# Two stages of an fp32 layer pair move to three rounded products, and the rows of a third product move to ScalarE and GpSimd

## Chip, core and metric

One core of one Trainium2 chip. The metric is the device time of one execution of the kernel in microseconds (us), median of several runs; lower is better. The kernel before took 2692.47 us (2692.26 to 2692.58 in 3 runs).

## The reference, cut to what matters

The kernel computes three stacked layers in fp32 for 256 tokens of width 2048. Only the first layer is touched:

```
mod = silu(c) @ w_ada + b_ada                      # 1 x 6144
shift, scale, gate = split(mod, 3)
h = rms_norm(x) * (1 + scale) + shift              # 256 x 2048
xr, gr, qc, kvc, kr, ga = split(h @ w_in)          # xr, gr, ga: 1024 wide each
y_rnn = rg_lru_branch(xr, ...) * silu(gr)
y_att = mla_branch(qc, kvc, kr, ...) * silu(ga)    # 8 heads
x = x + gate * (concat(y_rnn, y_att) @ w_out)
```

Two later layers (a differential attention and a stick-breaking attention, each with a convolutional feed-forward) follow and are the same in both kernels. They take the stretch from about 455 us to the end.

## The kernel before, in words

Everything lies transposed: features on the 128 partitions, 256 tokens along the row. `xm` is h in the reference's sense (16 tiles of 128 features x 256 tokens, fp32), `h` is the residual stream x, of the same size.

**Units.** Weights arrive in units of 4 x 128 rows by 256 columns (512 KB, 128 partitions x 1024 numbers). In the first layer each unit lies in a ring of 8 places `w1`; TensorE multiplies it as plain fp32 (helper `two_tiles`, L838 to L846, and the loop at L1032 to L1042): 8 matmuls of 128x128 weights by 128x256 activations. The profile shows an fp32 matmul as two records. The units run in this order, counted by the semaphore `w1_used`: up to unit 39 the modulated latent products and three quarters of the recurrent products; units 40 to 43 the last quarter of xr (L995 to L998); units 44 to 57 the fourteen pairs of heads of the latent attention, `U_PAIRS` (nope, rope, knope, v; L1002 to L1011); units 58 to 61 the last quarter of gr; units 62 to 77 the attention gate ga, four groups of four units. From unit 58 on, after each unit comes `attention(slot)` (L1014), which puts in a head's scores, turns and outputs, and in slots 3 and 19 `gate_sums` (L982).

In all later products a unit is split instead: ScalarE copies it rounded (`hi`, L1367), VectorE subtracts the copy from it (L1841), and TensorE takes high times high, high times low and low times high, in type float32r. The first split units are those of `w_out` (`residual_product`, L1115 and L1173), right behind unit 77. Their wide form lets one matmul of 512 columns carry two of the three products.

**Gate rows.** The gate third of `mod` isn't needed before `w_out`'s results are added up. It is made on VectorE in 32 rows (`gate_row`, L2131): one row is 128 of the 2048 rows of w_ada by 1024 columns, loaded by SyncE's queue into one of the four places of `raw` (`gate_load`, L542; it waits until the row 4 before has been used), and VectorE multiplies it by silu(c) of its partition and adds it to `gate_sum` in one instruction (L2144, L2141 for the first of each half). After 16 rows `gate_sums` adds up over the partitions on TensorE with 8 matmuls (L989), then `gate_sum` is used again for the other half.

**Queues.** Each engine runs its instructions in the order written. ScalarE (L1455 to L1581) takes in the pairs: the logarithm and exponential of the roots of the pair before (L1416, L1418), the squares of this pair (L1496), for v a copy (L1498) and the sigmoids of the recurrent gates (L1483). VectorE (L2148 to L2279) has the latent outputs, four convolutions (`conv`, L2109), `rnn_in` (L2097), heads (L2121), gate rows between them; then per head the maxima, a step of the recurrence, the weights of the head, two gate rows. GpSimd does nothing after two kinds of memsets at the start (L666, L668). SyncE's queue issues all loads in the order of use.

The lines that set the path of the pairs are these three waits of TensorE:

```
two_tiles(halves(take(U_BANK[n], read=(F.heads_out.sem, 2 + n) ...)), ...)   # a bank is free again
head_sums(n - 1)                                                             # waits for ScalarE's squares of pair n-1
recurrent_gates(g)                                                           # waits for ScalarE to have read scores and turned
```

Of the kernel before, what the change touches and what calls it, by code (L numbers as in the profile page):

```python
# [16 lines left out]
F32 = mybir.dt.float32  # L17
# [64 lines left out]
for _n in range(ONE_UNITS):  # L82
    _lora = _n < XR_AT and not any(q <= _n < q + 8 for q in QUARTER_AT)
    _size = LORA_COLS if _lora else UK * 256
    if _n == ONE_UNITS - 8:
        _at = ONE_SPACE // 2
    if _at + _size > ONE_SPACE:
        _at = 0
    ONE_SPAN.append((_at, _at + _size))
    _at += _size  # L90

ONE_FREE = [max([m + 1 for m in range(n) if ONE_SPAN[m][0] < ONE_SPAN[n][1] and ONE_SPAN[n][0] < ONE_SPAN[m][1]]
                + [n - ONE_RING + 1, 0]) for n in range(ONE_UNITS)]
# [136 lines left out]
def splits(units):  # L230
# [8 lines left out]
     "ada_product"]  # L239
# [4 lines left out]
class FirstBlock:  # L244


    def __init__(self, sems):
# [3 lines left out]
         self.pack_in, self.ada_product, *slots) = [Tally(s) for s in sems]  # L251
# [20 lines left out]
FIRST_SLOT = 2  # L272
# [34 lines left out]
def program(nc, t, out, consts):  # L307

    ctx = ExitStack()
    with ctx:  # L310
# [17 lines left out]
        h = sb("h", [KT, TOK])  # L328
        begin_at("weights_gap", WEIGHTS_STEP)
        wr_at = nc.sbuf_base  # L330
        wr = sb("wr", [2, SLOT_PAIR], F32R)
        w1 = nc.alloc_sbuf_tensor_at("w1", [P, ONE_SPACE], F32, offset=-(-wr_at // 32) * 32)
# [36 lines left out]
        xm = nc.alloc_sbuf_tensor_at("xm", [P, KT, TOK], F32, offset=xs_at)  # L369
        half = nc.alloc_sbuf_tensor_at("half", [P, KT, TOK], F32, offset=xs_at + KT * TOK * 4)  # L370
        gate_sum = nc.alloc_sbuf_tensor_at("gate_sum", [P, GATE_COLS], F32, offset=xs_at + KT * TOK * 4)
# [23 lines left out]
        rgw = o("rgw", [2, 8, P])  # L395
        p1 = [o(f"p{e}", [3 * P]) for e in range(2)]
# [55 lines left out]

        def lora_rows(n):

            return w1[:, ONE_SPAN[n][0]:ONE_SPAN[n][0] + LORA_COLS]
# [17 lines left out]
        def _(sp):  # L473
# [33 lines left out]
            ada_loads, one_units, gate_loads = [0], [0], [0]  # L507
# [34 lines left out]
            def gate_load():  # L542

                n = gate_loads[0]
                gate_loads[0] += 1
                if n >= RING:
                    sp.wait_ge(T.gate_used.sem, n - RING + 1)
                r, c = n % KT, 2 * D + (n // KT) * GATE_COLS
                sp.dma_start(raw[:, n % RING, :], w_ada[r * P:(r + 1) * P, c:c + GATE_COLS])\
                  .then_inc(F.gate_in[n % RING].sem, 16)  # L550

# [34 lines left out]
            sp.wait_ge(F.rgw_zeroed.sem, 1)  # L586
            for m, name in enumerate(("w_rg_a", "w_rg_x")):
                for b in range(2):
                    r = slice(64 * b, 64 * b + 64)
                    sp.dma_start(rgw[r, m, :, r], t[name][0].rearrange("(t b) i j -> b i t j", b=2)[b])\  # L590
                      .then_inc(T.rgw_in.sem, 16)
            for i in range(4):
                quarter_load(i, 3)
            for what, g in U_PAIRS:
# [8 lines left out]
                gate_load()  # L603
            for i in range(4):
                quarter_load(4 + i, 3)
                gate_load()
            for n in range(N_GA):
                pair_load(GA + 256 * (n // 4), n % 4)
                if n < GATE_LOADS - N_U - 4:
                    gate_load()  # L610
# [19 lines left out]
            for n in range(8):  # L630
                cols = slice(n * 256, (n + 1) * 256)
                pair(w_out, cols)

# [29 lines left out]
        def _(pool):  # L663
            F = FirstBlock(first_sems)
# [3 lines left out]
            pool.memset(rgw[:, :, :, :], 0.0).then_inc(F.rgw_zeroed.sem, 1)  # L668


        @block.tensor
        def _(pe):
# [174 lines left out]

            def halves(b):
# [133 lines left out]
            def gate_sums(step):  # L982
# [5 lines left out]
                for m in range(n):  # L988
                    mm = pe.matmul(sums[:, step * n + m:step * n + m + 1], gate_sum[:, m * P:(m + 1) * P], ones[:, 0:1],  # L989
# [10 lines left out]
            pe.wait_ge(T.rgw_in.sem, 64)  # L1000

            for n, (what, g) in enumerate(U_PAIRS):  # L1002
                if g == 0:
# [10 lines left out]
            def attention(slot):  # L1014
# [8 lines left out]
                if slot == 3:  # L1023
                    gate_sums(0)
                if slot == 19:
# [3 lines left out]
            for i in range(4):  # L1029
                two_tiles(halves(take(GR_BANK[i])), xm, 3 * UK)  # L1030
# [1591 lines left out]
```

## Time and profile before

| | before |
|---|---|
| median of 3 runs | 2692.47 us |
| the profiled execution, its own time | 2691.99 us |
| its span, first to last instruction | 2689.8 us |
| busy: PE / DVE / ACT / POOL | 2679.5 / 1977.5 / 1197.8 / 5.7 us |
| DMA, mean share of 16 engines | 64% of the span, 528 MB |

PE is TensorE, DVE VectorE, ACT ScalarE, POOL GpSimd, SP SyncE; a name with q behind it is the engine's queue of DMA issues. L12 is line 12 of the kernel before. The profiled execution's time holds 2.2 us around the span. Durations of matmuls overlap in the rows, since they are pipelined: what one costs is read from start to start.

### The profile page before, as it was taken

The page shows a single profiled execution, that of the slowest core. Times are in us where ns is not written, and L with a number is a line of the kernel's source. Part 1 is how long each engine was busy: PE and PEld are TensorE (multiplying, and loading weights), DVE is VectorE, ACT ScalarE, POOL GpSimd, SP SyncE. Part 2 cuts the span into 40 slices and gives each one's busy share as a digit, 9 for nine tenths or more (in the row PEclk, how much of TensorE's full clock was granted, in tenths as well). Part 3 has the DMA queues.
Part 4 walks back from the last instruction along what each step waited for, and adds up shares of the span by engine and source line. Part 5 has one row for each costly group of instructions (what it writes and reads, how often), then busy time and mean ns, then how long its engine had stood idle before and what let it go on. Part 6 is the DMA issues. An engine that isn't in the chain of part 4 may idle for free.

```text
span 2689.8 us, 44167 instructions
## 1 busy us (share of the span) xinstructions
PE 2679.5 (100%) x15336; PEld 2348.9 (87%) x15336; DVE 1977.5 (74%) x2594; ACT 1197.8 (45%) x1533; POOL 5.7 (0%) x12
## 2 busy tenths in 40 slices
PE   9999999999999999999999999999999999999999
PEld 7888888888888888888888888888888888888888
DVE  6747577777777788667787776699878876688865
ACT  2004354555555444444444443366544444444443
POOL 0000000000000000000000000000000000000000
PEclk9999999999999999999999999999999999999999
DMA  9986665555556666666666666644566666666664
GB/s 342 366 278 191 205 192 191 165 174 163 160 164 196 188 195 190 198 190 195 189 194 188 196 200 190 188 157 140 181 188 195 196 191 192 192 190 195 196 202 155
DMA packets 705780, 528.18 MB, mean 196 GB/s; under 512 B 32221, under 2 KB 694559, under 8 KB 705439
## 3 DMA queue, kind: packets, MB, share of 16 engines
q1 hardware_dynamic: 701872, 523.73, 63.9%
q10 hardware_dynamic: 3823, 3.31, 0.4%
q8 instruction: 54, 0.88, 0.1%
q14 instruction: 31, 0.25, 0.0%
HBM read 523.80 MB, written 2.10 MB: 196 GB/s over the span
## 4 chain that ended last, share of the span: by engine, by line
PE 97%; DVE 2%; ACT 1%; issue 0%; DMA 0%; DVEq 0%; SPq 0%; ACTq 0%
PE acc L707 80%; PE acc L845 3%; PE acc L1039 2%; PE acc L833 2%; PE turned L845 2%; PE sums L845 2%; PE mixed L960 1%; PE sums L1191 1%; DVE pro_ada L1915 0%; DVE wr L1841 0%; PE scores L1184 0%; PE sums L745 0%; PE mixed L961 0%; PE sums L916 0%; PE scores L946 0%
## 5 line engine op out<-in xcount | busy, mean ns | idle before, releaser
L707 PE MATMUL acc<-stream,wr 128*128 128x512 f32 (+1 forms) x7680 | 1328.4, 333 | 0.3 <-DVE wr L1841 0.3
L707 PEld LDWEIGHTS acc<-stream,wr 128*128 128x128 f32 x7680 | 1159.1, 188 | 156.0 <-issue 3.8
L1841 DVE TENSOR_TENSOR wr<-raw,wr 128x1024 fp32r<-128x1024 f32 x832 | 998.5, 1222 | 318.2 <-ACT wr L1367 308.6
L1367 ACT ACTIVATE wr<-raw 128x1024 fp32r<-128x1024 f32 x832 | 871.1, 1058 | 693.8 <-PE acc L707 678.1
L707 PE MATMUL acc<-ys,wr 128*128 128x512 f32 (+1 forms) x4264 | 732.4, 332 | 1.0 <-DVE wr L1841 0.9
L707 PEld LDWEIGHTS acc<-ys,wr 128*128 128x128 f32 x4264 | 642.7, 188 | 85.3 <-DVE wr L1841 1.5
L707 PE MATMUL acc<-wr,stream 128*128 128x512 f32 (+1 forms) x1024 | 182.7, 338 | 0.0
L707 PEld LDWEIGHTS acc<-wr,stream 128*128 128x128 f32 x1024 | 157.0, 188 | 22.5 <-issue 0.5
L1725 ACT ACTIVATE ffn_cv<-ffn_cv 128x256 f32<-128x256 f32 x88 | 36.9, 419 | 245.4 <-DVE ffn_cv L2459 245.4
L1851 DVE TENSOR_REDUCE ffn_ug<-acc 128x512 f32<-128x1024 f32 x88 | 107.8, 1225 | 35.3 <-PE acc L707 35.3
L1874 DVE TENSOR_TENSOR ys<-tmp,ys 128x256 f32 (+3 forms) x108 | 51.2, 474 | 76.0 <-ACT ys L1373 73.4
L1915 DVE SCALAR_TENSOR_TENSOR pro_ada<-aring,small,pro_ada 128x512 f32<-128x512 f32 (+1 forms) x103 | 85.7, 832 | 24.3 <-DMA aring<-in_w_ada 18.3
L1851 DVE TENSOR_REDUCE S<-acc 128x512 f32<-128x1024 f32 x71 | 86.6, 1220 | 12.1 <-PE acc L707 12.1
L1373 ACT ACTIVATE ys<-tmp 128x256 f32 (+3 forms) x104 | 46.8, 450 | 106.3 <-DVE tmp L2463 102.0
L1855 DVE TENSOR_TENSOR ffn_ug<-ffn_ug,rx 128x512 f32<-128x512 f32 x88 | 60.9, 692 | 3.0
L833 PE MATMUL acc<-xm,w 128*128 128x256 f32 x256 | 58.2, 381 | 0.4 <-DVE xm L1935 0.4
L1039 PE MATMUL acc<-xm,w 128*128 128x256 f32 x256 | 57.3, 379 | 0.0
L833 PEld LDWEIGHTS acc<-xm,w 128*128 128x128 f32 x256 | 48.2, 190 | 8.3 <-issue 1.9
L1039 PEld LDWEIGHTS acc<-xm,w 128*128 128x128 f32 x256 | 47.7, 190 | 6.0
L2457 DVE SCALAR_TENSOR_TENSOR ffn_cv<-ffn_ug,vcol,ffn_cv 128x256 f32<-128x256 f32 x88 | 42.7, 485 | 13.2 <-DVE ffn_cv L2454 13.0
L2459 DVE SCALAR_TENSOR_TENSOR ffn_cv<-ffn_ug,vcol,ffn_cv 128x256 f32<-128x256 f32 x88 | 42.7, 485 | 13.0 <-DVE ffn_cv L2457 12.8
L2454 DVE TENSOR_SCALAR ffn_cv<-ffn_ug,vcol 128x256 f32<-128x256 f32 x88 | 36.3, 413 | 16.6 <-DVE ffn_ug L1855 16.4
(334 smaller groups left out, 1546.1 us busy)
## 6 DMA issues: line engine op xcount, KB each, us to landing
raw<-in_ffn_w_up SPq DMA_DIRECT2D x704, 256.0 KB
raw<-in_ffn_w_down SPq DMA_DIRECT2D x160, 512.0 KB
raw<-in_a_w_qkv SPq DMA_DIRECT2D x96, 512.0 KB
raw<-in_b_w_kv SPq DMA_DIRECT2D x64, 512.0 KB
aring<-in_w_ada SPq DMA_DIRECT2D x96, 256.0 KB, 6.6
w<-in_w_in SPq DMA_DIRECT2D x48, 512.0 KB
raw<-in_w_ada SPq DMA_DIRECT2D x32, 512.0 KB, 5.1
raw<-in_w_out SPq DMA_DIRECT2D x32, 512.0 KB
```

The lines of the kernel that those rows point to most:

```text
L707: mm = pe.matmul(*ops, start=first and ops is wide, stop=last and ops is wide)
L833: pe.matmul(bank(c // 2)[:, (c % 2) * TOK:(c % 2 + 1) * TOK], w[:, c * P:(c + 1) * P], xm[:, k, :], start=False, stop=k == KT - 1 and c % ...
L845: mm = pe.matmul(out(j), *here, start=k == 0, stop=k == UK - 1)
L1039: mm = pe.matmul(bank(b + j)[:, 0:TOK], w[:, k, j * P:(j + 1) * P], xm[:, u * UK + k, :], start=u == 0 and k == 0, stop=u == 3 and k == UK ...
L1367: f(half_of(0, s), raw[:, s, :], ACT.Copy)\
L1373: f(to[0], to[1], ACT.Copy).then_inc(T.hi_out.sem, 1)
L1841: tt(half_of(1, s), raw[:, s, :], half_of(0, s), ALU.subtract).then_inc(T.unit_split[s].sem, 1)
L1851: dve.tensor_reduce(out_tiles, a[:, 0:tiles, :].rearrange("p t (b c) -> p t c b", b=2), axis=AX_X, op=ALU.add)\
L1855: tt(out_tiles, out_tiles, both(rx), ALU.mult).then_inc(*T.acc_read.one())
L1874: tt(to[:, :, TOK:2 * TOK], src, to[:, :, 0:TOK], ALU.subtract).then_inc(*T.lo_out.one())
L1915: stt(here, aring[:, n % ADA_RING, 0:2 * kn * P], small[:, 8 + r:9 + r], here, ALU.mult, ALU.add)\
L2457: step(stt(cv[e][:, :], UG[e][:, 1, 1:1 + TOK], taps[1], cv[e][:, :], ALU.mult, ALU.add))
```

## The change

1. The products of units 58 to 77 (last quarter of gr, whole ga) are made from three rounded products of 128x256 each, 24 float32r matmuls a unit instead of 8 fp32 ones. ScalarE makes the rounded copy of each unit (`high`), VectorE the rest (`low`, written over the unit itself). The activations are split too: `xm_high` (4 instructions of ScalarE) and `xm_low` (4 of VectorE, written over `xm`).
2. `xm_high` takes the place of `h`. So `h` is stored to memory (2 MB, on ScalarE's queue, which waits for the landing) and fetched back by SyncE's queue in four pieces, behind units 74 to 77.
3. The gate rows leave VectorE. GpSimd issues their loads (from unit 32 on), ScalarE scales each row in place (7 ahead of the latent squares, then 2 with each pair, 1 less at the end), GpSimd adds it to one of two `gate_sum` tiles, waits for its own addition, and issues the load of the row 4 further on. `gate_sums` move to slots 0 and 10.
4. The recurrent weights are loaded behind unit 50 rather than before unit 40; VectorE's first convolution moves up; the first split slot of `w_out` is 0 rather than 2.

The places of `w1` from unit 58 on are five for units and three for the rounded copies. The core of the diff:

```diff
-for _n in range(ONE_UNITS):
+for _n in range(GR_AT):
...
+LOW_PLACES, HIGH_PLACES = [5, 6, 0, 1, 2], [7, 4, 3]
+ONE_FREE = [max(users_of(ONE_SPAN[n], n) + [n - ONE_RING + 1, 0]) for n in range(ONE_UNITS)]
+HIGH_FREE = [max(users_of(HIGH_SPAN[n], n)) if n >= GR_AT else 0 for n in range(ONE_UNITS)]
...
-FIRST_SLOT = 2
+FIRST_SLOT = 0
...
         @block.gpsimd
+            pool.wait_ge(F.w1_used.sem, XR_AT - 7)
+            def gate_load(n):
+                r, c = n % KT, 2 * D + (n // KT) * GATE_COLS
+                pool.dma_start(raw[:, n % RING, :], t["w_ada"][0][r * P:(r + 1) * P, c:c + GATE_COLS])\
+                    .then_inc(F.gate_in[n % RING].sem, 16)
+            for n in range(RING):
+                gate_load(n)
+            for n in range(GATE_LOADS):
+                r = n % KT
+                here = gate_sum[n // KT][:, :]
+                pool.wait_ge(F.gate_scaled.sem, n + 1)
+                if r:
+                    w = pool.tensor_tensor(here, here, raw[:, n % RING, :], ALU.add)
+                else:
+                    w = pool.tensor_copy(here, raw[:, n % RING, :])
+                w.then_inc(T.gate_used.sem, 1)
+                pool.wait_ge(T.gate_used.sem, n + 1)
+                if n + RING < GATE_LOADS:
+                    gate_load(n + RING)
...
         @block.tensor
+            def three_products(out, high, low, j, k, k0, first, last):
+                cols = slice(j * P, (j + 1) * P)
+                x_high, x_low = xm_high[:, k0 + k, :], xm_low[:, k0 + k, :]
+                pe.matmul(out, high[:, k, cols], x_high, start=first, stop=False)
+                pe.matmul(out, high[:, k, cols], x_low, start=False, stop=False)
+                return pe.matmul(out, low[:, k, cols], x_high, start=False, stop=last)
...
-                if slot == 3:
+                if slot == 0:
                     gate_sums(0)
-                if slot == 19:
+                if slot == 10:
                     gate_sums(1)
...
         @block.scalar
-                        act.wait_ge(F.w1_used.sem, ONE_UNITS if s < FIRST_SLOT else ONE_UNITS - 4)
+                        act.wait_ge(F.w1_used.sem, ONE_UNITS - 2 if s < RING // 2 else ONE_UNITS)
...
+            act.wait_ge(F.w1_used.sem, QUARTER_AT[2])
+            act.dma_start(h_kept, h[:, :, :]).then_inc(F.h_kept.sem, 16)
+            act.wait_ge(F.h_kept.sem, 16)
+            act.wait_ge(F.xm_ready.sem, KT)
+            for u in range(4):
+                f(xm_high[:, u * UK:(u + 1) * UK, :], xm[:, u * UK:(u + 1) * UK, :], ACT.Copy).then_inc(F.high_ready.sem, 1)
+            def gate_scale(count):
+                for _ in range(count):
+                    n = gate_rows[0]
+                    gate_rows[0] += 1
+                    act.wait_ge(F.gate_in[n % RING].sem, 16 * (n // RING + 1))
+                    f(raw[:, n % RING, :], raw[:, n % RING, :], ACT.Copy, scale=small[:, 8 + n % KT:9 + n % KT])\
+                        .then_inc(F.gate_scaled.sem, 1)
+            gate_scale(7)
+            def high(count=1):
+                for _ in range(count):
+                    n = high_units[0]
+                    high_units[0] += 1
+                    act.wait_ge(F.w1_in[n % ONE_RING].sem, UNIT * (n // ONE_RING + 1))
+                    act.wait_ge(F.w1_used.sem, HIGH_FREE[n])
+                    f(high_tiles(n), unit_tiles(n), ACT.Copy).then_inc(F.high_out.sem, 1)
...
                 if what != "v":
                     f(flat(sq[n % 2][:, :, :]), bank(U_BANK[n]), ACT.Square).then_inc(F.sq_ready.sem, 1)
+                    gate_scale(2)
...
+                    if n < N_U - 1:
+                        gate_scale(2 if g < 2 else 1)
             gates(3)
+            high()
...
         @block.vector
-                elif n:
-                    gate_row()
-                if n >= N_U:
-                    gate_row()
+                    tt(low_tiles(n), unit_tiles(n), high_tiles(n), ALU.subtract).then_inc(F.low_out.sem, 1)
...
-                gate_row()
-                gate_row()
+                low(2 if hd < 7 else 1)
...
+            dve.wait_ge(F.h_back.sem, 4 * 16)
             residual_product(gated=True, gain=VEC["attn_norm_g_2"])
```

## Rows read from the trace of the kernel before

**Rows 1.** Busy us by stretch: PE, PEld, DVE, ACT, POOL, clock, DMA share, GB/s.

```profile
207.00:270.00 63.00, 63.00 (x270) 50.95 (x269) 45.15 (x64) 26.04 (x46) 0.00 (x0) 1.00 0.69 210
288.00:367.00 79.00, 79.00 (x397) 65.62 (x396) 55.52 (x103) 32.08 (x69) 0.00 (x0) 1.00 0.59 188
```

**Rows 2.** PE in order of time, attention gate: one unit is 16 records.

```profile
304.90 3.62 PE L1039 MATMUL acc<-xm,w 128*128 128x256 f32 x16
308.35 0.59 PE L960 MATMUL mixed<-one_pT,one_v 128*128 128x256 f32 x2
```

**Rows 3.** PE in order of time at the kernel's end: float32r matmuls of 256 columns.

```profile
2671.20 0.28 PE L733 MATMUL acc<-wr,ys 128*128 128x256 f32 x1
...
2672.14 0.28 PE L735 MATMUL acc<-wr,ys 128*128 128x256 f32 x1
```

**Rows 4.** Groups by line, whole kernel: the splitting of a unit on DVE and ACT.

```profile
L1841 DVE TENSOR_TENSOR wr<-raw,wr 128x1024 fp32r<-128x1024 f32 x832 | 998.5, 1222 | 318.2 <-ACT wr L1367 308.6
L1367 ACT ACTIVATE wr<-raw 128x1024 fp32r<-128x1024 f32 x832 | 871.1, 1058 | 693.8 <-PE acc L707 678.1
```

**Rows 5.** Groups by line on POOL, shapes kept apart; and DVE's gate rows.

```profile
L668 POOL MEMSET one_rgw<- 128x2048 f32 x1 | 1.8, 1810 | 17.9 <-PE turned L778 17.9
L666 POOL MEMSET pro_ada<- 128x1024 f32 x1 | 1.0, 958 | 0.0
...
L2144 DVE SCALAR_TENSOR_TENSOR gate_sum<-raw,small,gate_sum 128x1024 f32<-128x1024 f32 x30 | 38.5, 1282 | 4.0 <-DMA raw<-in_w_ada 2.5
```

**Rows 6.** DMA issues by line (KB each, us to landing), and two issues on SP's queue.

```profile
raw<-in_w_ada SPq DMA_DIRECT2D x32, 512.0 KB, 5.1
...
230.82 0.34 SPq L549 DMA_DIRECT2D raw<-in_w_ada  x1
...
269.06 0.94 SPq L549 DMA_DIRECT2D raw<-in_w_ada  x1
```

**Rows 7.** ACT, DVE and PE in order of time where the latent squares are made.

```profile
173.26 0.73 DVE L1935 TENSOR_SCALAR xm<-xm,mod 128x256 f32<-128x256 f32 x2
...
188.50 1.08 ACT L1457 ACTIVATE sq<-acc 128x512 f32<-128x512 f32 x2 [104.30 <-PE scores L835]
...
191.76 1.89 PE L906 MATMUL mixed<-sq,ones 128*128 128x256 f32 x8
```

**Rows 8.** ACT and PE in order of time in the pairs of heads.

```profile
210.09 0.60 ACT L1496 ACTIVATE sq<-acc 128x512 f32<-128x512 f32 x1 [6.42 <-PE acc L845]
...
223.02 0.69 ACT L1416 ACTIVATE rs<-sums,epsc 128x512 f32<-128x512 f32 x1 [1.37 <-PE sums L916]
223.74 0.63 ACT L1418 ACTIVATE rs<-rs 128x512 f32<-128x512 f32 x1
224.28 0.58 ACT L1496 ACTIVATE sq<-acc 128x512 f32<-128x512 f32 x1
...
266.15 0.84 ACT L1483 ACTIVATE ri<-scores,vcol 128x256 f32<-128x256 f32 x2 [0.27 <-PE scores L978]
...
222.82 3.62 PE L845 MATMUL acc<-qx,w 128*128 128x256 f32 x16
...
227.13 3.62 PE L845 MATMUL acc<-qx,w 128*128 128x256 f32 x16
...
270.26 1.03 PE L978 MATMUL scores<-xc,one_rgw 128*128 128x256 f32 x4
```

**Rows 9.** DVE and PE in order of time at the fourth pair's bank.

```profile
217.58 0.69 DVE L2097 TENSOR_TENSOR xrp<-acc,half 128x512 f32<-128x512 f32 x1
...
218.51 3.62 PE L845 MATMUL acc<-qx,w 128*128 128x256 f32 x16
```

**Rows 10.** PE in order of time behind the attention gate, and one more stretch of busy time.

```profile
367.41 1.84 PE L989 MATMUL sums<-ones,gate_sum 128*128 128x1 f32 x16
369.12 26.14 PE L707 MATMUL acc<-ys,wr 128*128 128x512 f32 x152
...
145.00:188.00 43.00, 43.00 (x209) 38.07 (x208) 20.54 (x34) 0.00 (x0) 0.00 (x0) 1.00 0.87 270
```

More of the change, by code:

```diff
@@ L90, with users_of @@
     _at += _size
-ONE_FREE = [max([m + 1 for m in range(n) if ONE_SPAN[m][0] < ONE_SPAN[n][1] and ONE_SPAN[n][0] < ONE_SPAN[m][1]]
-                + [n - ONE_RING + 1, 0]) for n in range(ONE_UNITS)]
+LOW_PLACES, HIGH_PLACES = [5, 6, 0, 1, 2], [7, 4, 3]
+HIGH_SPAN = [None] * GR_AT
+for _n in range(ONE_UNITS - GR_AT):
+    for _spans, _place in ((ONE_SPAN, LOW_PLACES[(_n + 2) % 5]), (HIGH_SPAN, HIGH_PLACES[_n % 3])):
+        _spans.append((_place * UK * 256, (_place + 1) * UK * 256))
+def users_of(span, n):
+    return [m + 1 for m in range(n) for used in (ONE_SPAN[m], HIGH_SPAN[m])
+            if used and used[0] < span[1] and span[0] < used[1]]
+ONE_FREE = [max(users_of(ONE_SPAN[n], n) + [n - ONE_RING + 1, 0]) for n in range(ONE_UNITS)]
+HIGH_FREE = [max(users_of(HIGH_SPAN[n], n)) if n >= GR_AT else 0 for n in range(ONE_UNITS)]
 XR_BANK, U_BANK, GR_BANK = [None, None, 0, 1], [(n + 2) % 4 for n in range(N_U)], [0, 1, 2, 3]
@@ L585, in _ @@
                 lora_load(k)
[L586 to L591, printed above, removed]
             for i in range(4):
                 quarter_load(i, 3)
-            for what, g in U_PAIRS:
+            for n, (what, g) in enumerate(U_PAIRS):
                 if what in ("nope", "rope"):
@@ L999, in _ @@
             rope_turn(kpe[:, :], 1, 0)
-            pe.wait_ge(T.rgw_in.sem, 64)
             for n, (what, g) in enumerate(U_PAIRS):
+                if what == "v" and g == 0:
+                    pe.wait_ge(T.rgw_in.sem, 64)
                 if g == 0:
@@ L1029, in _ @@
             for i in range(4):
-                two_tiles(halves(take(GR_BANK[i])), xm, 3 * UK)
+                out = halves(take(GR_BANK[i]))
+                high, low = split_unit()
+                for j in range(2):
+                    for k in range(UK):
+                        mm = three_products(out(j), high, low, j, k, 3 * UK, k == 0, k == UK - 1)
+                mm.then_inc(F.w1_used.sem, 1)
                 attention(i)
@@ L1491, in _ @@
                     act.preload_act_table(ACT.Sigmoid)
+                if n == N_U - 1:
+                    high(2)
                 if what == "v" and g:
@@ L2127, in rope_out, with xm_lows, low @@
                             F.mixed_ready, F.mixed_read))
-            gate_rows = [0]
-            def gate_row():
-                n = gate_rows[0]
-                gate_rows[0] += 1
-                r = n % KT
-                if n == KT:
-                    dve.wait_ge(T.gate_summed.sem, 1)
-                dve.wait_ge(F.gate_in[n % RING].sem, 16 * (n // RING + 1))
-                c = small[:, 8 + r:9 + r]
-                if r == 0:
-                    w = ts(gate_sum[:, :], raw[:, n % RING, :], c, None, ALU.mult)
-                else:
-                    own(T.gate_used)
-                    w = stt(gate_sum[:, :], raw[:, n % RING, :], c, gate_sum[:, :], ALU.mult, ALU.add)
-                w.then_inc(*T.gate_used.one())
+            def xm_lows(u):
+                tiles = slice(u * UK, (u + 1) * UK)
+                dve.wait_ge(F.high_ready.sem, u + 1)
+                tt(xm_low[:, tiles, :], xm[:, tiles, :], xm_high[:, tiles, :], ALU.subtract)
+            low_units = [GR_AT]
+            def low(count=1):
+                for _ in range(count):
+                    n = low_units[0]
+                    low_units[0] += 1
+                    dve.wait_ge(*F.high_out.next())
+                    tt(low_tiles(n), unit_tiles(n), high_tiles(n), ALU.subtract).then_inc(F.low_out.sem, 1)
+            for u in range(3):
+                xm_lows(u)
             lora_out("q")
             rnn_in(0)
+            conv(0)
             lora_out("kv")
+            rnn_in(1)
             rope_key()
-            conv(0)
-            rnn_in(1)
             dve.wait_ge(T.table_ready.sem, 4)
@@ L2246, in _ @@
             F.scores_ready.n, F.scores_read.n = 8, 8
-            for i in range(4):
+            for i in range(3):
+                low()
                 rnn_gate(i)
```

73 lines of the change are left out of this document (50 added, 23 removed).

## The prediction

> **What bounds the kernel now.** I read the busy time by stretch first [rows 1]: TensorE is busy in every microsecond of the two stretches the change touches (63.00 of 63 us in the pairs of heads, 79.00 of 79 in the attention gate, clock 1.00), while VectorE has 45.15 and 55.52, ScalarE 26.04 and 32.08 and GpSimd nothing. So TensorE's own work is the path, and the others matter where they make it wait. Then the order of time on TensorE [rows 2, 3] for the price of a product, the groups by line [rows 4, 5] and the DMA issues [rows 6] for the price of what is added, and the order of time on ScalarE beside TensorE [rows 7, 8] for how late ScalarE may be before TensorE waits.
>
> **The product.** A plain unit runs from 304.90 to the next operation's start at 308.35: 3.45 us for 8 fp32 matmuls, 0.43 each [rows 2]. Float32r matmuls of 256 columns with new weights each stand at the end of the kernel: 8 steps from 2671.20 to 2672.14, 0.118 us each [rows 3]. Three products are 24 of them a unit: 2.83 us. Twenty units (58 to 77) give 20 x 0.62 = **-12.5 us**, all on the path, since TensorE has no idle time there. The ends: 0.118 is of the same shape and type, so no better; if the new places in the memory read more slowly, at worst the whole gain is gone (0).
>
> **What carries the splits.** ScalarE's rounded copy takes 1.06 us, VectorE's subtraction 1.22 [rows 4]. In the attention gate (15 of the 20 units' splits fall there, the others earlier) ScalarE gets 32.1 + 15 x 1.06 = 48 us, VectorE 55.5 - 15 gate rows x 1.28 [rows 5] + 15 x 1.22 = 54.6 us, both in a stretch that shrinks to some 69. Both fit. TensorE has two units of lead on the splits, so a wait comes from order only: I take +1. The sums of the gate's second half (1.7 us from 367.41 to 369.12 [rows 10]) move to slot 10 and cost the same there, but no longer cover the first splits of the output product: +1. Together **+2** (0 to 4).
>
> **The gate rows** are the doubtful part. Their 32 instructions leave VectorE, which was not the bound: worth nothing by itself. In their place each row passes ScalarE (1.06 us in the queue that makes the squares TensorE waits for), then GpSimd's addition, then GpSimd's issue of the load four rows on, then 5.1 us to landing [rows 6]. The ring has four places, and ScalarE's `gate_scale` waits for the landing with squares, roots and sigmoids queued behind it. So the number that decides is c, GpSimd's time per row, addition plus issue. No row shows either. The nearest: GpSimd writes 1024 numbers per partition in 0.958 us (2048 in 1.81) [rows 5]. An addition reads two streams and writes one: 0.96 if all overlap, 2.87 if they come one behind the other. The issue: SyncE's queue takes 0.34 us for the same transfer free of pressure and 0.94 with it [rows 6]. c lies between 1.3 and 3.8. I take three streams in a row and the free issue, 2.87 + 0.34 = **3.2**: the same instruction on VectorE, the faster engine for it in these rows, already takes 1.28 with two inputs, so full overlap on GpSimd is unlikely.
>
> *First wait.* `xm` is complete at 173.26 + 0.73 = 174.0 [rows 7]; four copies of xm take ScalarE to 178.2, row 0 is scaled by 179.3. GpSimd issues rows 4, 5, 6 at 3.2 us each (row 0 is a copy, one stream or 0.96 less): row 6 at 187.9, landed 193.0, scaled 194.1. The latent squares started at 188.50, so they are 5.6 late. They took 1.08, and TensorE asked at 191.76 [rows 7]: 2.2 of cover. Price **+3.4**.
>
> *The pairs.* One pair lasts 4.31 us on TensorE (222.82 to 227.13) [rows 8]. ScalarE's own part is 0.72 + 0.63 + 0.58 us (starts 223.02, 223.74, 224.28) and now two scalings, 2.12: 4.05 of 4.31, so ScalarE alone still keeps up. GpSimd needs 6.4 us for the two rows, and it stood still before, because row 7 is only scaled behind the squares of pair 0: those ended at 210.7 [rows 8], with the shift 214.1, row 7 scaled at 215.2. Row 31's load is issued after 21 additions (rows 7 to 27): 215.2 + 21 x 3.2 = 282.4, less 0.96 for row 16, a copy: 281.4. Landed 286.5, scaled 287.6, and behind it the first sigmoid of the recurrent gates (0.84 us; it began at 266.15) ends at 288.4. TensorE's next gates stood at 270.26 [rows 8], with the shift 273.7. Price **+15**, seen as waits of some 2 us in nearly each pair. It is late at squares first, then at sigmoids.
>
> **Shared port.** GpSimd's additions now run beside VectorE's convolutions. VectorE's `rnn_in` for the bank of the fourth pair ended at 218.27, TensorE took the bank at 218.51 [rows 9]: 0.24 us of cover, some 2 more from the convolution moved up. If VectorE must let additions pass there (at most two, 2 x 2.87), it costs 0 to 6; no gain, since nothing here frees VectorE before that point. I take **+3**, the middle. The Trainium skill, page SBUF — State Buffer, section "Who interferes with whom", says that a VectorE instruction with two SBUF inputs and a GpSimd instruction that reads SBUF block each other for the whole instruction, whoever comes second; by it the top end counts, without it 0. No row here has both engines at it.
>
> **At nothing.** The store of `h` (2 MB) and four early row loads fall between 143 and 172 us, where DMA is at 0.87 and 270 GB/s [rows 10]: 4 MB are some 13 us of transfers against 43 x 0.13 = 5.6 us free, but the loads there run two to five units ahead of TensorE, which hides them (0 to +3 if not). ScalarE waits for the store's landing, but was idle for 104.30 us before 188.50 [rows 7]. `xm_high` and `xm_low` (4 x 1.06, 3 x 1.22) fall into the same idle time. The four issues that fetch `h` stand on SyncE's queue ahead of the loads of `w_out`'s second columns; these are needed four units, 11 us, later, and 2 MB take about 7. The recurrent weights' four issues move behind unit 50, over 20 us ahead of their use. If that cover is gone it is 1 to 2 us once.
>
> **Sum.** -12.5 + 2 + 3.4 + 15 + 3 = +10.9. Against the profiled execution (2691.99, of which 2689.8 are span) that is 2702.9; the median is 0.5 above that execution: 2703.
>
> **Rivals.** A measurement of this kernel tells some 0.2% (5.4 us) from no change.
>
> *A, faster: the ring keeps up.* Each 0.1 us of c weighs 24 x 0.1 = 2.4 us, and the sum is zero at c = 3.2 - 10.9 / 24 = 2.75; below 2.5 it is faster by over 0.2%. With c = 1.3 row 6 is scaled within the 2.2 us of cover and nothing waits: -12.5 + 2 = -10.5, or 2682. For it: GpSimd's writing is as quick as ScalarE's copy. Against: two inputs. With VectorE undisturbed and c about 1.9, 2683. Chance 0.24.
>
> *B, no change.* GpSimd's addition takes twice VectorE's 1.22 [rows 4], the issue 0.34: c = 2.8, -9.6 on the forecast, 2693. Chance 0.15. The page GPSIMD Engine Reference, section 3.1, gives 4497 ns for such an addition of 2048 numbers, an estimate of 2.25 us for 1024; with the issue as above, c would be 2.6 and the time 2689. The same skill's page DMA: Bandwidth & Descriptors, section "Latency and other measured facts", gives about 1 us until the first byte of a transfer issued by GpSimd, which would bring c back to 3.3. No row here shows either.
>
> *C, slower still.* The issue costs as much as SyncE's under pressure, c = 3.8: +1.8 at the first wait, +12.6 in the pairs, and the port's top end, +3: 2720. Half-way lies the case that the three products don't bring what they say, for the places of `xm_high` and the copies read more slowly: at worst +12.5, 2715. Chance 0.19.
>
> Forecast (c from 2.9 to 3.6, 2698 to 2713): 0.42.
>
> **How the numbers follow.** Faster is A, 0.24; same is B, 0.15; slower is the forecast and C, 0.61. The range goes from A's likely end, 2683, to just above C's, 2722; about a tenth is left on each side. The forecast's own range is 2698 to 2713.
>
> **What would show it.** On TensorE, units 58 to 77 start 2.83 us apart where no attention lies between. GpSimd's start-to-start time from one addition to the next between 215 and 280 us is c. ScalarE's scalings show idle time ended by the rows' DMA; TensorE waits for ScalarE at L916 in most pairs, and at L978. VectorE's convolutions show whether they wait beside GpSimd. I am wrong if c is under 2.7, if ScalarE's waits stay inside TensorE's cover, or if units 58 to 77 take over 3 us.

## The result, and the profile after

| | before | after |
|---|---|---|
| median | 2692.51 us (4 runs) | 2707.95 us (2707.05 to 2710.44, 4 runs) |
| ratio to before | | 1.0058, interval 1.0046 to 1.0071 |
| the profiled execution, and its span | 2691.99, 2689.8 us | 2708.8, 2707.0 us |
| busy PE / DVE / ACT / POOL | 2679.5 / 1977.5 / 1197.8 / 5.7 us | 2676.6 / 1990.9 / 1255.3 / 97.8 us |

The change makes the kernel 15.4 us slower; 2703 was forecast, with 2683 to 2722 as the range. In the experiments below one execution of e3 (7382.36 us) and one of e10 (3339.08 us) were slow; the medians given for these two include it and would otherwise be 2686.86 and 2697.69 us.

Busy time by stretch in the kernel after (columns as in [rows 1]):

```profile
207.00:270.00 63.00, 52.22 (x207) 40.35 (x205) 45.29 (x45) 35.49 (x46) 45.10 (x32) 0.95 0.78 228
220.00:226.00 6.00, 0.87 (x3) 0.04 (x1) 5.93 (x4) 0.51 (x1) 5.66 (x4) 0.99 0.83 269
226.00:232.00 6.00, 4.35 (x10) 3.50 (x11) 4.28 (x7) 2.36 (x4) 0.68 (x2) 0.50 0.38 121
276.00:282.00 6.00, 0.53 (x3) 0.13 (x1) 0.75 (x1) 4.79 (x7) 5.36 (x5) 0.87 0.51 150
282.00:286.00 4.00, 3.71 (x9) 3.02 (x10) 0.00 (x0) 2.52 (x5) 3.58 (x3) 0.50 0.65 198
290.00:370.00 80.00, 79.41 (x571) 71.51 (x570) 52.65 (x89) 52.58 (x98) 7.18 (x3) 0.98 0.46 134
```

In the pairs of heads TensorE, busy without a gap before [rows 1], now lacks 10.8 of 63 us. Two holes stand out, 220 to 226 and 276 to 282, and behind each the granted clock is 0.50, the 1.2 GHz level. From 290 us on, where the three products run, hardly anything is lost: the clock of 0.98 there is a fall to 0.66 between 346 and 350 us, and the version without rows (e4 below) has the same fall at 322 to 326 us. So the loss lies in the pairs, as forecast. The list of waits between 150 and 400 us (us in total, times, longest) names what TensorE waited for:

```profile
PE acc L892 <- DVE xrp L2203: 6.8, 1, 6.8
PE scores L1040 <- ACT ri L1580: 5.8, 1, 5.8
PE sums L978 <- ACT sq L1595: 4.2, 2, 2.3
PE mixed L968 <- ACT sq L1554: 1.4, 1, 1.4
PE acc L906 <- DVE w_split L2250: 1.0, 2, 0.5
PE acc L754 <- DVE wr L1947: 0.6, 2, 0.3
ACT raw L1537 <- DMA raw<-in_w_ada: 18.2, 13, 2.6
```

The last row is the ring of four rows: ScalarE's scaling stood 13 times for a transfer, 18.2 us in all. What sets the pace of the ring is GpSimd's order of time in the pairs (start, us, operation):

```profile
238.48 0.57 POOL L699 DMA_DIRECT2D raw<-in_w_ada  x1 [0.30 <-POOL gate_sum L709]
239.08 2.37 POOL L709 TENSOR_TENSOR gate_sum<-gate_sum,raw 128x1024 f32<-128x1024 f32 x1
241.74 0.57 POOL L699 DMA_DIRECT2D raw<-in_w_ada  x1 [0.30 <-POOL gate_sum L709]
242.34 2.36 POOL L709 TENSOR_TENSOR gate_sum<-gate_sum,raw 128x1024 f32<-128x1024 f32 x1
```

One row costs 2.37 for the addition, 0.30 in which GpSimd stands before it issues the next load, and 0.57 for the issue: c = 3.26 us from start to start, where 3.2 was taken. The first entry of the waits, though, is VectorE's. This is the convolution ahead of it, beside TensorE, in order of time:

```profile
210.83 2.71 DVE L2215 SCALAR_TENSOR_TENSOR xc<-xrp,vcol,xc 128x256 f32<-128x256 f32 x6
213.65 0.69 DVE L2203 TENSOR_TENSOR xrp<-acc,half 128x512 f32<-128x512 f32 x1
214.38 2.46 DVE L2213 TENSOR_SCALAR xc<-xrp,vcol 128x256 f32<-128x256 f32 x2
216.88 9.93 DVE L2215 SCALAR_TENSOR_TENSOR xc<-xrp,vcol,xc 128x256 f32<-128x256 f32 x6
226.90 0.69 DVE L2203 TENSOR_TENSOR xrp<-acc,half 128x512 f32<-128x512 f32 x1
...
227.65 6.19 PE L892 MATMUL acc<-qx,w 128*128 128x256 f32 x16 [6.78 <-DVE xrp L2203]
233.68 1.02 PE L978 MATMUL sums<-sq,ones 128*128 128x512 f32 x2
```

The same six instructions take 2.71 us at 210.83, while GpSimd waits for a row, and 9.93 at 216.88, while it adds. `xrp` comes 9.3 us later than in [rows 9], TensorE stands 6.78 us, and its next unit lasts 6.03 us from start to start (227.65 to 233.68) in place of 3.45: 2.58 more for the clock. The second hole costs 5.76 and then 2.54 (7.72 from 282.29 to 290.01 for what takes 5.18 from there to 295.19). With the other waits that is 19.8 of waiting and 5.1 of clock.

VectorE is behind one more of these waits, although the list names ScalarE's squares for it. The convolution after that one, on VectorE, ScalarE and TensorE:

```profile
232.62 9.51 DVE L2215 SCALAR_TENSOR_TENSOR xc<-xrp,vcol,xc 128x256 f32<-128x256 f32 x6
242.06 0.74 DVE L2227 SCALAR_TENSOR_TENSOR one_qn<-acc,vcol,rs 128x512 f32<-128x512 f32 x1
242.89 0.69 ACT L1483 ACTIVATE rs<-sums,epsc 128x512 f32<-128x512 f32 x1 [4.24 <-DVE one_qn L2227]
244.15 0.58 ACT L1595 ACTIVATE sq<-acc 128x512 f32<-128x512 f32 x1
244.78 1.13 PE L978 MATMUL sums<-sq,cst 128*128 128x512 f32 x2 [2.32 <-ACT sq L1595]
```

The head's output `one_qn` stands behind the stretched convolution, ScalarE waits 4.24 us for it before it takes the next root, the squares stand behind that root, and TensorE waits 2.32 us. ScalarE waits for no row's transfer between 191.6 and 252 us. Its waits for transfers come again from 252 us on, ahead of the other wait at the squares (1.90 us at 270.22) and of the 5.76 at the sigmoids.

### The profile page after: what moved, and what is told of

Same layout as the page of the kernel before. It is cut to its first block, busy times and chain, and to the rows that moved or that the text cites. A ratio compares the mean times of both kernels' runs of the same rounds, so it can differ in the third digit from the quotient of the medians.

```text
span 2707.0 us, 44576 instructions
## 1 busy us (share of the span) xinstructions
PE 2676.6 (99%) x15496; PEld 2349.5 (87%) x15496; DVE 1990.9 (74%) x2586; ACT 1255.3 (46%) x1589; POOL 97.8 (4%) x76
## 4 chain that ended last, share of the span: by engine, by line
PE 92%; DVE 4%; ACT 1%; POOL 1%; issue 1%; DMA 1%; DVEq 0%; SPq 0%; ACTq 0%; POOLq 0%
PE acc L754 80%; PE sums L892 2%; PE turned L892 1%; PE acc L880 1%; POOL gate_sum L709 1%; DVE xc L2215 1%; PE mixed L1022 1%; PE sums L1258 1%; PE acc L892 1%; PE acc L906 0%; DVE wr L1947 0%; PE acc L908 0%; PE acc L907 0%; PE scores L1251 0%; PE sums L792 0%
## 5 line engine op out<-in xcount | busy, mean ns | idle before, releaser
L1957 DVE TENSOR_REDUCE S<-acc 128x512 f32<-128x1024 f32 x71 | 86.7, 1221 | 11.7 <-PE acc L754 11.7
L709 POOL TENSOR_TENSOR gate_sum<-gate_sum,raw 128x1024 f32<-128x1024 f32 x30 | 71.8, 2394 | 19.6 <-ACT raw L1537 18.7
L880 PE MATMUL acc<-xm,w 128*128 128x256 f32 x256 | 58.3, 380 | 0.4 <-DVE xm L2041 0.4
L880 PEld LDWEIGHTS acc<-xm,w 128*128 128x128 f32 x256 | 48.2, 190 | 8.3 <-issue 1.9
L2250 DVE TENSOR_TENSOR w_split<-w,w_split 128x1024 fp32r<-128x1024 f32 x20 | 27.0, 1381 | 35.0 <-ACT w_split L1550 35.0
```

The source lines that it names most:

```text
L709: w = pool.tensor_tensor(here, here, raw[:, n % RING, :], ALU.add)
L880: pe.matmul(bank(c // 2)[:, (c % 2) * TOK:(c % 2 + 1) * TOK], w[:, c * P:(c + 1) * P], xm[:, k, :], start=False, stop=k == KT - 1 and c % ...
L1957: dve.tensor_reduce(out_tiles, a[:, 0:tiles, :].rearrange("p t (b c) -> p t c b", b=2), axis=AX_X, op=ALU.add)\
```

## Experiments

They ran in three groups, each beside the kernel before on the same chip (2692.4 to 2692.5). Two theories stood against each other. **Ring:** only the time of a row counts, through the landing of the row four places on. **Port:** GpSimd's addition also holds up VectorE's instructions with two operands from SBUF. Where a version is told as e1, e2 and so on, that is its number below.

**e4: no rows (what the products alone are worth).** 30 of the 32 rows are neither loaded, scaled nor added (the attention's gate is left out of the result).

```diff
-            gate_scale(7)
+            gate_scale(2)
...
-                    gate_scale(2)
-                        gate_scale(2 if g < 2 else 1)
```

> Thirty of the 32 gate rows are left out (their loads, scalings and additions; the two rows left are copied). What stays is the three products, the split of the activations, the store and return of h, the moved loads. All theories on the rows: 2680 to 2684, the products' 12.5 us less some 1 to 3 for order and tail. If 2690 or more, the products or the store of h cost more than I think and the rows' part is smaller.

Measured: 2682.88 us (2682.45 to 2685.5), ratio 0.9965 (0.9953 to 0.9978). TensorE's whole list of waits between 150 and 400 us is:

```profile
PE acc L899 <- DVE w_split L2240: 1.1, 2, 0.6
PE acc L747 <- DVE wr L1937: 0.6, 2, 0.3
```

So the rows and what carries them cost 25.1 us in the changed kernel (2707.95 - 2682.88). In the two profiled executions the difference is 24.1 (2708.8 - 2684.74), and the waits (19.8 - 1.7) with the clock (5.1) give 23.2 of it.

**e8: the kernel before without the rows.** The control for e4: 30 of 32 rows left out of the kernel before, in loads and sums.

```diff
             def gate_row():
                 n = gate_rows[0]
                 gate_rows[0] += 1
+                if n % KT:
+                    return
```

> The kernel before with 30 of its 32 gate rows left out, loads and sums (the gate of attention is left out of the result). If the rows hide completely beside the fp32 products, it takes 2692 us as before, and the 9.5 us between before and the version of the changed kernel without rows are the worth of the products alone. If the rows and their loads cost something there, it is faster by that, up to 2 us, and the products are worth so much less.

Measured: 2692.34 us (2691.93 to 2692.78), ratio 0.9999 (0.9990 to 1.0008). On VectorE, beside fp32 products, the rows were free, and the three products with all that goes with them are worth 9.5 us (2692.4 - 2682.9).

**e1: GpSimd only writes.** The addition becomes memsets of 1024, 1024 and 256 numbers, which read nothing (the gate is left out of the result).

```diff
-                    w = pool.tensor_tensor(here, here, raw[:, n % RING, :], ALU.add)
+                    pool.memset(raw[:, n % RING, :], 0.0)
+                    pool.memset(here, 0.0)
+                    w = pool.memset(scratch[:, :], 0.0)
```

> GpSimd's additions become three memsets of 1024, 1024 and 256 numbers (about 2.2 us by its memset rows, 2.4 for the addition), which write and read nothing; what is left out is the sum itself. GpSimd's time per row stays about 3.1 us, so the ring of rows is as slow as before the edit. Theory ring (ScalarE waits for rows, TensorE for ScalarE, and that is the whole loss): 2703 to 2706, nearly all of the loss stays. Theory port (GpSimd's reading blocks VectorE's convolutions, and that is the loss): VectorE's convolution group L2215 back at 2.7 us from 9.9, TensorE's wait of 6.8 us for xrp gone, 2681 to 2685. Theory both in a row: the 6.8 us and some 2.5 us of slow clock behind it go, the waits at squares and sigmoids grow by part of that, 2695 to 2700.

Measured: 2694.73 us (2693.68 to 2696.94), ratio 1.0010 (1.0000 to 1.0019), at 2.93 us a row: next to the range of "both", far from the other two. Groups by line between 170 and 300 us, VectorE's convolutions:

```profile
L2218 DVE SCALAR_TENSOR_TENSOR xc<-xrp,vcol,xc 128x256 f32<-128x256 f32 x24 | 10.6, 482 | 0.4
L2216 DVE TENSOR_SCALAR xc<-xrp,vcol 128x256 f32<-128x256 f32 x8 | 4.6, 616 | 0.1
```

The 24 instructions take 10.6 us in all, as in the kernel before; no wait for `xrp` is left, and the clock is 1.00 from 207 to 290 us. GpSimd was busy for 62.46 of those 83 us, more than in e2 below (55.67). So it isn't GpSimd's being busy that holds VectorE up. (The second row, 4.6 in place of 2.9 before, shows that one kind is slowed by writes as well: see the last section.)

**e2: ScalarE doesn't scale.** GpSimd waits for the transfer itself, so ScalarE is out of the ring (the scale is left out of the result).

```diff
-                pool.wait_ge(F.gate_scaled.sem, n + 1)
+                pool.wait_ge(F.gate_in[n % RING].sem, 16 * (n // RING + 1))
```

> ScalarE scales no row (left out: the product with silu(c)); GpSimd waits for the landing itself and adds, 3.26 us a row, in one run from about 165 us on. Theory ring: no wait of TensorE at squares or sigmoids is left, 2682 to 2686. Theory port: the additions now run beside all four convolutions from 199 us on, the wait for xrp stays at 6 to 9 us or comes earlier, 2690 to 2695. Both: 2690 to 2695, with all that is left of the loss at waits for VectorE.

Measured: 2720.43 us (2719.44 to 2720.86), ratio 1.0102 (1.0085 to 1.0119). With less work than the changed kernel it is 12.5 us slower. GpSimd and VectorE of this kernel in order of time (starts 3.25 us apart for the additions):

```profile
201.48 2.36 POOL L711 TENSOR_TENSOR gate_sum<-gate_sum,raw 128x1024 f32<-128x1024 f32 x1
204.14 0.57 POOL L699 DMA_DIRECT2D raw<-in_w_ada  x1 [0.30 <-POOL gate_sum L711]
204.72 2.37 POOL L711 TENSOR_TENSOR gate_sum<-gate_sum,raw 128x1024 f32<-128x1024 f32 x1
...
201.11 9.90 DVE L2217 SCALAR_TENSOR_TENSOR xc<-xrp,vcol,xc 128x256 f32<-128x256 f32 x6
210.94 1.65 DVE L2184 SCALAR_TENSOR_TENSOR kvx<-acc,vcol,rs 128x256 f32<-128x256 f32 x4
212.51 0.67 DVE L2205 TENSOR_TENSOR xrp<-sums,half 128x512 f32<-128x512 f32 x1
```

Three additions pass during the six instructions (9.90 = 3 x 3.25, nearly), so two of the six go with each addition. Taken one by one they last 3.02, 0.47, 2.82, 0.47, 2.81 and at most 0.5 us: one passes in the gap of 0.89 us between additions, and the next, which starts before the addition (at 204.56 ahead of 204.72, the first at 201.11 ahead of 201.48), lasts until the addition is over. The additions themselves stay at 2.36 us. The instructions behind them, which take one operand from an accumulator bank, run beside the next addition at their usual 0.41 and 0.67 us. The theory of the ring alone falls here: the ring had lost ScalarE's part and the kernel went up. TensorE's waits were 11.4 us for `xrp`, 8.2 for `sq` and 6.8 for `kpe`; behind that `sq` ScalarE had waited 12.18 us for `one_qn`, after a convolution of 11.99. The forecast of the port had only the time wrong (2690 to 2695).

**e3: a copy in place of the addition.** One operand read in place of two.

```diff
-                if r:
-                    w = pool.tensor_tensor(here, here, raw[:, n % RING, :], ALU.add)
-                else:
-                    w = pool.tensor_copy(here, raw[:, n % RING, :])
+                w = pool.tensor_copy(here, raw[:, n % RING, :])
```

> GpSimd copies each scaled row (one operand read, one written) in place of adding it to the sum (two read, one written): the gate of attention is left out of the result. The changed kernel showed such a copy at 1.05 us against 2.37 us for an addition, so a row should take 1.05 + 0.30 + 0.57 = 1.9 us. Theory ring (only the time of a row counts): the ring keeps up, 2684 to 2687 us. Theory port (GpSimd holds up VectorE's instructions with two operands whenever it reads): the copies still hold VectorE up, but for 1.05 of every 1.9 us and only while rows are in work; six of the convolution's instructions in a row take between 2.7 and 7 us, and the kernel 2685 to 2692 us. If only an instruction of GpSimd with two operands read holds VectorE up, the six take 2.7 us as in the kernel before.

Measured: 2686.88 us, ratio 0.9979 (0.9969 to 0.9989). GpSimd and VectorE in order of time:

```profile
223.27 1.04 POOL L708 COPY gate_sum<-raw 128x1024 f32<-128x1024 f32 x1 [1.96 <-ACT raw L1534]
225.13 1.05 POOL L708 COPY gate_sum<-raw 128x1024 f32<-128x1024 f32 x1
227.07 1.22 POOL L708 COPY gate_sum<-raw 128x1024 f32<-128x1024 f32 x1
...
223.34 5.22 DVE L2212 SCALAR_TENSOR_TENSOR xc<-xrp,vcol,xc 128x256 f32<-128x256 f32 x6
```

A single operand read is enough: the six take 5.22 us, 2.5 more than undisturbed, beside copies that fill 1.05 of every 1.9 us. The stretch falls where "any read" had put it, and "only two operands read" is out. The time doesn't tell the theories apart, since 2686.88 lies in the ranges of both ring and port. In TensorE's waits the port doesn't show directly: 1.3 us at the sigmoids and 0.4 at the squares, and ScalarE had waited 1.11 us for a row's transfer ahead of the latter.

**e7: SyncE issues the loads.** GpSimd's row loses its 0.57 us of issue; all else is as changed.

```diff
-                if n + RING < GATE_LOADS:
-                    gate_load(n + RING)
...
         @block.sync
+                gate_loads_before(n + 1)
```

> The changed kernel, but SyncE issues the loads of the gate rows in place of GpSimd: a row costs GpSimd 2.37 + 0.30 us instead of 3.26 us. Theory ring: at 2.7 us a row the ring nearly keeps pace and ScalarE's rows come in time, 2686 to 2693 us. Theory port: GpSimd now adds for 2.37 of every 2.7 us while rows are in work, VectorE's convolutions take at least as long as in the changed kernel (six in a row 9 us or more), TensorE waits again for xrp or qn, and the kernel takes 2700 to 2712 us.

Measured: 2705.85 us (2702.63 to 2707.11), ratio 1.0045 (1.0030 to 1.0060). The convolution of the third quarter in VectorE's order of time:

```profile
215.08 4.63 DVE L2227 TENSOR_SCALAR xc<-xrp,vcol 128x256 f32<-128x256 f32 x2
219.75 6.76 DVE L2229 SCALAR_TENSOR_TENSOR xc<-xrp,vcol,xc 128x256 f32<-128x256 f32 x6
226.61 0.69 DVE L2217 TENSOR_TENSOR xrp<-acc,half 128x512 f32<-128x512 f32 x1
```

The row got shorter than expected: where GpSimd doesn't wait for a row its additions start 2.43 us apart (180.85, 183.28, 185.71), although it still waits for its own addition, so the 0.30 us belong to the issue behind it. By the forecast's own rate (2.4 us for each 0.1 us of c) 0.83 less should have brought some 20 us; 2.1 came. `xrp` is done at 227.3, 0.3 us earlier than in the changed kernel. With the gap between additions gone, VectorE's place to slip through is gone too: beside additions in a row each of its instructions lasts about one addition (2.19 and 2.52 for the first two here), and the next convolution takes 11.06 us. TensorE waits 5.8 us for `xrp` and 4.4 for squares that stand behind that next convolution. The forecast of the port holds (2700 to 2712), though the six at this place took 6.76, not 9 or more.

**e10: writes only, but longer rows.** e1 with one more wait inside the row.

```diff
-                    pool.memset(raw[:, n % RING, :], 0.0)
+                    pool.memset(raw[:, n % RING, :], 0.0).then_inc(F.pool_step.sem, 1)
+                    pool.wait_ge(F.pool_step.sem, n - n // KT)
```

> As the version in which GpSimd only writes (three memsets for an addition, 2.93 us a row, 2694.7 us), with one more wait inside each row, so that a row takes the 3.25 us of the changed kernel and still reads nothing (the gate of attention is left out). Theory ring alone: the row's time is all that counts, 2704 to 2710 us. Theory both (the ring and the reads): 0.3 us more on some 25 rows is at most 8 us, 2698 to 2703 us, and the rest to 2708 us is what GpSimd's reads do to VectorE, with the slower clock that follows. TensorE's clock stays at full speed and no wait for xrp appears in either version without reads.

Measured: 2697.91 us (2696.33 at the lowest), ratio 1.0020 (1.0010 to 1.0029). My setting missed its mark: a row took 3.05 us (217.90, 220.94, 223.99 in GpSimd's order of time), not 3.25, for a wait on GpSimd's own signal costs about 0.1 us where no issue follows. The rate from e1 to here is 3.2 us for 0.12, or 2.7 for each 0.1, close to the forecast's 2.4. Carried on to 3.26 at 2.4 it gives 2703, which is an extrapolation. One expectation was wrong: the clock did fall here (0.96 from 207 to 290 us), behind waits for `sq` of up to 3.2 us, with no read of GpSimd's anywhere.

**e5, e6, e9: the products kept, the rows back on VectorE.** These compute all that the reference asks. e5 puts VectorE's own row instruction (scaled and added in one, 1.28 us) at two a pair, with SyncE's loads among the units:

```diff
-            gate_scale(7)
...
+                elif n:
+                    gate_row(1 if n < 3 else 2)
```

> Complete kernel: the products as changed, the rows again one fused instruction of VectorE each (1.28 us), but two with each pair from the fifth on, one behind each of the first three lows and heads; loads on SyncE's queue four rows ahead; ScalarE and GpSimd have no part in them. Ring and port theories alike: both causes are gone, 2681 to 2686, faster than both kernels. If VectorE is now too full, it shows as waits of TensorE for low_out or for heads, 2690 to 2700.

Measured: 2690.10 us, ratio 0.9994 (0.9984 to 1.0003): 18 us better than the change, and no better than before. The forecast was missed; TensorE's waits were 3.7 us at the sigmoids and 1.4 for the transfer of `w_uq`. e6 takes six rows ahead of the latent sums and gives five to the heads:

```diff
             for u in range(3):
                 xm_lows(u)
+            gate_row(6)
...
-                    gate_row(1 if n < 3 else 2)
+                    gate_row(2 if 3 < n < 8 else 1)
```

> As the version with the rows back on VectorE (2690.1 us), but with six rows done by VectorE right after the low parts of xm, where it stood idle for 16 us and the DMA engines had nothing to do for 20 us a little later, and fewer rows beside the units of the value heads, where the DMA engines had been busy all the time. If late transfers are the 7 us that separated that version from the one without rows (2682.9 us), it takes 2683 to 2686 us, and TensorE waits neither for w_uq nor for the recurrent gates. If VectorE's own time is the cost, it stays at 2688 to 2691 us.

Measured: 2688.06 us (2686.5 to 2688.89), ratio 0.9983 (0.9974 to 0.9992): half a miss. The wait for the gates was gone, but the one for `w_uq` was not (1.8 us), and the heads had a new one of 1.4. SyncE's order of time showed why: it stood ahead of `w_uq` until VectorE freed a row's place at 219.3 us. e9 issues the rows one unit later there and moves two rows from the heads to the pairs:

```diff
-            rows_by = [6, 7, 8, 8, 10, 12, 14, 16] + [17 + i for i in range(11)] + [27, 28]
+            rows_by = [6, 6, 7, 8, 10, 12, 14, 16, 18, 20] + [21 + i for i in range(8)]
```

> As the last version with the rows on VectorE (2688.1 us), in which TensorE still waited 1.8 us for w_uq, because SyncE stood at the load of a row whose place VectorE freed only at 219.3 us, and 1.4 us for a head's probabilities, where VectorE had five rows among the heads. Here SyncE issues the rows one unit later, and two rows move from the heads to the pairs. If these two waits are the difference, it takes 2684 to 2686 us; if the rows cost something that no wait of TensorE shows, it stays at 2687 to 2688 us.

Measured: **2682.99 us (2682.31 to 2684.37), ratio 0.9966 (0.9953 to 0.9978)**: 9.5 us faster than the kernel before, 25 us faster than the change, and a little better than its forecast. It equals e4, which has 2 rows of the 32. Busy time by stretch:

```profile
207.00:290.00 83.00, 82.18 (x414) 68.63 (x413) 63.24 (x82) 41.52 (x77) 0.00 (x0) 1.00 0.79 254
```

and its waits of TensorE between 150 and 400 us:

```profile
PE acc L893 <- DMA w<-in_w_ukv: 0.8, 1, 0.8
PE acc L907 <- DVE w_split L2236: 0.7, 2, 0.5
PE acc L755 <- DVE wr L1933: 0.6, 2, 0.3
PE mixed L1023 <- ACT one_pT L1623: 0.2, 1, 0.2
```

The 32 rows are back to costing nothing, beside products that are now faster.

## Why the prediction was right

The sign, the mechanism and most terms held: slower, 15.4 us against 10.9. Term by term:

- **The product, -12.5, with order and tail +2.** Measured together -9.5 (e4 against e8), where -10.5 was forecast. The unit's price is a little over the forecast's 2.83 us: the first matmul of a unit takes 0.2 to 0.3 us until the next starts, not 0.118, so an undisturbed unit of the kernel after lasts 2.89 (TensorE in order of time):

```profile
326.11 0.37 PE L906 MATMUL acc<-xm_high,w_split 128*128 128x256 f32 x1
326.32 0.28 PE L907 MATMUL acc<-xm_low,w_split 128*128 128x256 f32 x1
326.44 0.28 PE L908 MATMUL acc<-xm_high,w_split 128*128 128x256 f32 x1
...
329.00 0.59 PE L1022 MATMUL mixed<-one_pT,one_v 128*128 128x256 f32 x2
```

  20 x 0.56 = 11.2; of that, 1.0 goes into the waits for `w_split` and 0.6 into those for `wr`. The +2 for both was right.
- **c = 3.2 us.** It measured 3.26, but two of the parts were off and cancelled: the addition is 2.37 (2.87 taken), the issue 0.57 (0.34 taken), and the 0.30 ahead of the issue stood in no step of the sum. That 3.2 came out so near is luck.
- **First wait, +3.4.** The squares started at 192.67, 4.2 after those in [rows 7] (5.6 forecast), and TensorE waited 1.4 us. The term was 2 us too high: row 6 was issued 0.3 us earlier (187.58) and landed in 4.0 us, not 5.1, and TensorE itself asked 0.75 later, at 192.51.
- **The pairs, +15.** Without any read, the ring costs 11.8 us at 2.93 us a row (e1 - e4) and 15.0 at 3.05 (e10 - e4), first wait included. The forecast's 18.4 for both terms at 3.2, brought down by its own 2.4 per 0.1, gives 11.9 and 14.8. The rate and the level are confirmed for a ring without reads, as nearly as these runs can tell. It was to show as "waits of some 2 us in nearly each pair": that was wrong. One wait of 1.9 us at the squares and one of 5.8 at the sigmoids did it, and 5.1 us of the loss, 2.5 of them behind the sigmoids, is the clock, which the forecast had nowhere.
- **Shared port, +3 (0 to 6).** This is the step that was mis-sized. The forecast let "at most two" additions pass at one place. In truth every convolution that meets additions is stretched: three additions passed in one of them, the wait was 6.8 us and the clock behind it 2.6, 9.4 at that place alone, and the next convolution (9.51 us) brought the 2.3 us at the squares, 11.7 together. Its net share of the 15.4 is less, since TensorE's standing there gives the ring time to catch up: between 5 us (against e10 carried on to 3.26) and 10 (against e10 as it ran). The two convolutions before ran their six at 2.71 only because GpSimd stood from 201 to 214 us, waiting for ScalarE; e2 shows the price when it doesn't.
- **At nothing.** No wait of TensorE in the kernel after or in e9 names the store of `h`, the fetch of it or the recurrent weights.

With these terms -9.5 + 20 (ring at 3.26, first wait included, extrapolated) + 5 gives +15.5, but the 5 is the remainder to the measured time, so the sum tests nothing. Read place by place in the kernel after, the ring cost 1.4 + 1.9 + 5.8 and 2.5 of clock, 11.6 us, where 18.4 stood in the forecast, and the port 11.7, where 3 stood. Both readings hold: a ring without reads costs more than that (e1, e10), but in the kernel after TensorE's standing for VectorE gives the ring time to catch up. So that the time came within 5 us of the forecast is partly luck: two terms were off in opposite directions.

**The rivals.** A (the ring keeps up) needed c under 2.5 and a VectorE undisturbed. e3 has c = 1.9 and a VectorE that is still held up, and takes 2686.9, 4 us over e4; no wait of TensorE there is directly behind a convolution (1.3 us at the sigmoids, 0.4 at the squares), and how much of the 4 the port brings indirectly stays open. B took c = 2.8 as "no change"; e7 came to 2.4 and stayed at 2705.9, since with additions still in the way the time of a row is no longer what decides. C's top end for the port was the right size for the wait (6.8 us), in a sum whose issue it had too high (0.94 against 0.57). The section "Who interferes with whom" of the Trainium skill's page SBUF — State Buffer, cited in the forecast as speaking for the top end, agrees with every run on what contends with what: the two-operand instruction blocks against a read (2.71 to 9.93 us against an addition, 5.22 against a copy) and not against memsets (e1, 10.6 us for 24 as before). That it is the later one that stands, these traces don't bear out: in e2 VectorE's instruction starts by its record up to 0.37 us ahead of the addition's and still lasts until the addition's end (the records of GpSimd are rough, so this isn't settled). The other way round is seen too: beside a subtraction of VectorE's (128x1024) at 295.04 us an addition in the kernel after took 3.23 us. The Trainium skill's page GPSIMD Engine Reference, section 3.1, gives 4497 ns for an addition of 2048 numbers, an estimate of 2.25 us for 1024; the 2.37 measured are 5% more.

## What to carry to other kernels

Moving work to an idle engine buys nothing when the engine it leaves was not the bound (e8: the rows were free on VectorE), and may cost what the two engines share: before giving GpSimd a stream to read, look at which of VectorE's instructions with two operands from SBUF run beside it, and whether something waits behind them. A ring fed by three engines in turn runs at the pace of its slowest one, with the issue and what stands before it counted in (here GpSimd's 2.37 + 0.30 + 0.57 us; the whole turn, 1.15 for the scaling and 4.4 for the landing added, is 8.8 us over four places, or 2.2 a row, by estimate); write its steps down one by one and multiply by the number of rows that have to pass. And when a product gets faster, look for the time to hide the small work where the engines truly stand idle (here 16 us of VectorE ahead of the latent sums), with the issue order of the loads fixed to match.

## What the runs showed of the hardware

- **GpSimd's reads stop VectorE.** Six `scalar_tensor_tensor` instructions of 128x256 with two operands from SBUF: 2.71 us alone, 9.93 beside additions (2.37 on, 0.89 off), 5.22 beside copies (1.05 on, some 0.85 off), 2.71 beside memsets. I had expected it at one place of the kernel. Two of these short instructions (0.45 us each) go with each addition, one in the gap and one that lasts through the addition, and beside additions without a gap (e7) only one.
- **A write is enough for one kind.** `tensor_scalar` of 128x256, two in a row: 0.73 us alone, 2.46 beside additions, 0.99 to 2.15 beside memsets (e1, e10). The same section of the Trainium skill's page SBUF — State Buffer has VectorE's two-port modes contend with GpSimd in general; this fits it.
- **GpSimd's prices:** addition of 1024 numbers per partition 2.37 us, copy 1.04, memset 0.97, issue of a 512 KB load 0.53 to 0.57, with 0.30 of standing before it when it waits for GpSimd's own last instruction. The same kind of wait costs 0.07 us ahead of an addition (e7) and about 0.1 ahead of a memset (e10). VectorE with scale and addition in one: 1.28.
- **The clock's price of a hole.** Behind TensorE's waits of 6.78 and 5.76 us the granted clock read 0.50 (the 1.2 GHz level) in the next 6 and 4 us, and the work there took 2.58 and 2.54 us more than at full clock. These two waits thus cost about 40% more than the list of waits shows. Not every wait does so: in e1 one of 2.44 us left the clock at 1.00, in e10 one of 3.2 us was followed by 0.50. Nor does every fall have a wait ahead of it: in e4 the clock reads 0.64 from 322 to 326 us, where TensorE had been busy in every microsecond since 294. In e9, whose longest wait is 0.8 us, the clock is 1.00 from 207 to 290 us.
